# Even layer: VectorE's early operands in PSUM banks, and GLA outputs with tokens on partitions

## The reference, cut to what matters

```python
def _mix_even(h, past_k, past_v, past_ki, s0, w_in, q_norm, k_norm, rel_bias, gate_w2, gate_b2, gla_norm, w_out):
    q, k, v, qi, ki, wi, qb, kb, vb, rb, ab = _split(h @ w_in, EVEN_SIZES)
    q = _rmsnorm(q.reshape(bsz, L, A_HEADS, A_HEAD_DIM), q_norm)
    k = _rmsnorm(k.reshape(bsz, L, A_HEADS, A_HEAD_DIM), k_norm)
    ...
    o_a = _dsa_attention(...)                  # top-k selection, softmax, values
    log_alpha = jax.nn.log_sigmoid((ab @ gate_w2 + gate_b2).astype(jnp.float32)) / B_GATE_TAU
    o_b, s_new = _gla_chunked(qb * (B_KEY_DIM ** -0.5), kb, vb, log_alpha, s0, min(CHUNK, L))
    o_b = _rmsnorm(o_b.astype(h.dtype), gla_norm).reshape(bsz, L, B_VW) * jax.nn.silu(rb)
    out = jnp.concatenate([o_a.reshape(bsz, L, A_W), o_b], axis=-1) @ w_out
```

## Time and profile before

| | us |
|---|---|
| median of three runs | 1477.51 |
| lowest, highest | 1476.26, 1480.02 |
| the profiled execution | 1478.12 |
| its span in the trace | 1476.4 |
| PE busy in the span | 1423.6 (96%) |
| DVE, ACT, POOL busy | 896.6, 597.5, 370.6 |

### The profile page before, as it was taken

One profiled execution on the slowest core, in us unless ns is written; L12 is line 12 of the kernel. 1 busy time (PEld: TensorE's weight loads), 2 busy tenths in 40 slices (PEclk: granted clock), 3 DMA queues, 4 the chain that ended last, 5 costly groups with the idle time before them and its releaser, 6 DMA issues.

```text
span 1476.4 us, 25253 instructions
## 1 busy us (share of the span) xinstructions
PE 1423.6 (96%) x9708; PEld 1389.8 (94%) x9708; DVE 896.6 (61%) x1403; ACT 597.5 (40%) x975; POOL 370.6 (25%) x344
## 2 busy tenths in 40 slices
PE   7999999999779999999999999999999889999998
PEld 7999999999658999999999999989999779999998
DVE  5666655678755666655666655667565456666542
ACT  5333324446443433332433332558433544333322
POOL 4000024766415100012100003637766232000000
PEclk9999999999789999999999999989999999999999
DMA  7655951344202555864455684122222222555751
GB/s 186 179 158 146 285 146 42 116 129 139 87 3 87 143 144 157 210 178 97 123 158 145 167 228 117 58 86 87 59 85 58 90 85 82 155 157 147 185 149 44
DMA packets 324028, 188.23 MB, mean 127 GB/s; under 512 B 10954, under 2 KB 321352, under 8 KB 323964
## 3 DMA queue, kind: packets, MB, share of 16 engines
q1 hardware_dynamic: 322080, 183.22, 45.0%
q0 software_dynamic: 1216, 3.98, 0.9%
q10 hardware_dynamic: 668, 0.15, 0.1%
HBM read 183.22 MB, written 4.11 MB: 127 GB/s over the span
## 4 chain that ended last, share of the span: by engine, by line
PE 89%; DVE 6%; ACT 3%; issue 1%; DMA 1%; SPq 0%; ACTq 0%
PE PS L620 21%; PE PS L621 21%; PE PS L622 21%; PE PS L725 2%; PE PS L726 2%; PE PS L727 2%; PE PS L1193 2%; PE PS L1176 2%; PE PS L746 1%; PE PS L748 1%; PE PS L747 1%; PE PS L698 1%; PE PS L699 1%; PE PS L700 1%; DVE RA L2099 1%
## 5 line engine op out<-in xcount | busy, mean ns | idle before, releaser
L620 PE MATMUL PS<-h_hi,w_parts 128*128 128x320 f32 x1408 | 438.2, 311 | 7.1 <-DVE h_lo L1907 4.1
L621 PE MATMUL PS<-h_lo,w_parts 128*128 128x320 f32 x1408 | 436.4, 310 | 0.0
L622 PE MATMUL PS<-h_hi,w_parts 128*128 128x320 f32 x1408 | 436.3, 310 | 0.0
L620 PEld LDWEIGHTS PS<-h_hi,w_parts 128*128 128x128 f32 x1408 | 265.5, 189 | 8.8 <-issue 7.4
L621 PEld LDWEIGHTS PS<-h_lo,w_parts 128*128 128x128 f32 x1408 | 265.5, 189 | 0.3
L622 PEld LDWEIGHTS PS<-h_hi,w_parts 128*128 128x128 f32 x1408 | 265.4, 189 | 0.0
L1339 ACT ACTIVATE w_parts<-gu 128x1024 fp32r<-128x1024 f32 x176 | 176.6, 1050 | 158.4 <-PE PS L622 154.8
L620 PE MATMUL PS<-act_hi,w_parts 128*128 128x320 f32 x704 | 217.7, 309 | 0.0
L622 PE MATMUL PS<-act_hi,w_parts 128*128 128x320 f32 x704 | 217.6, 309 | 0.0
L621 PE MATMUL PS<-act_lo,w_parts 128*128 128x320 f32 x704 | 217.6, 309 | 0.0
L1895 DVE TENSOR_TENSOR w_parts<-gu,w_parts 128x1024 fp32r<-128x1024 f32 x176 | 209.1, 1229 | 3.4 <-ACT w_parts L1339 3.3
(11 more groups left out here) (386 smaller groups left out, 2380.5 us busy)
## 6 DMA issues: line engine op xcount, KB each, us to landing
gu<-in_ffn_w_gate SPq DMA_DIRECT2D x88, 512.0 KB, 4.0
gu<-in_ffn_w_up SPq DMA_DIRECT2D x88, 512.0 KB, 5.2
dn<-in_ffn_w_down SPq DMA_DIRECT2D x32, 1408.0 KB, 7.0
gu<-in_od_w_in SPq DMA_DIRECT2D x32, 512.0 KB, 5.0
gu<-in_ev_w_in SPq DMA_DIRECT2D x26, 512.0 KB, 4.8
dn<-in_ev_w_out SPq DMA_DIRECT2D x4, 1024.0 KB, 6.3
dn<-in_od_w_out SPq DMA_DIRECT2D x4, 1024.0 KB, 5.4
RB<-bias_rows POOLq DMA_DIRECT2D x2, 576.0 KB, 6.1
```

What stands on the lines that cost most here:

```text
L620: mm(out, w_hi, hi, start=first, stop=False)
L621: mm(out, w_hi, lo, start=False, stop=False)
L622: return mm(out, w_lo, hi, start=False, stop=last)
```

## The change

Two groups of edits, both in the even layer.

First, operands move from SBUF to PSUM. ScalarE's reciprocal roots stay in banks 4 to 7, where the sums were; VectorE reads them there for q and for k. VectorE's combined gate goes to banks 4 and 5, and the ten running sums read it there. Since the banks are held longer, three waits of TensorE change: `head_sums(4)` waits for the eight pieces of q, `gate()` for the four of k, `scores(0)` for `g_args`.

Second, `gla_outputs` swaps the two operands of each product, so that tokens (two heads by 64) are on partitions and the 128 features in columns. ScalarE squares each of the ten blocks from PSUM with an accumulated sum into `gcol`; the copy to `oT`, `gla_sums` and `gla_spread` are gone. VectorE scales the blocks by `gcol` (one instruction of 128x1280 into `o_rows`), TensorE turns them (ten transposes, `gla_turns`), and after `heads_out(3)` VectorE multiplies by gain and gate in four instructions (`gla_gated`). The factor 0.5 of the silu goes into the root (scale 0.25).

```diff
@@ TensorE @@
                     if l == 9:
-                        head_sums(4, s["qk_read"], 1)
+                        head_sums(4, s["q_ready"], 8)
...
             def gate():
-                pe.wait_ge(s["qk_read"], 2)
+                pe.wait_ge(s["k_ready"], 4)
...
-                        mm(PS[:, u * P:(u + 1) * P], vp[:, u, :], km_bd[:, p, c, :], start=True, stop=False)
-                        ins = mm(PS[:, u * P:(u + 1) * P], Sg(c if c < 4 else 5)[:, p, :], qe_bd[:, p, c, :],
+                        mm(PS[:, u * P:(u + 1) * P], km_bd[:, p, c, :], vp[:, u, :], start=True, stop=False)
+                        ins = mm(PS[:, u * P:(u + 1) * P], qe_bd[:, p, c, :], Sg(c if c < 4 else 5)[:, p, :],
                                  start=False, stop=True)
...
-                def gla_sums():
-                    pe.wait_ge(s["gsq"], 1)
+                def gla_turns():
+                    pe.wait_ge(s["o_rows"], 1)
                     for u in range(10):
-                        ins = mm(bank(2)[:, 256 + u:257 + u], o_squares[:, u * P:(u + 1) * P], ones[:, 0:1], start=True, stop=True)
-                    ins.then_inc(s["gsum"], 1)
-
-                def gla_spread():
-                    pe.wait_ge(s["grstd"], 1)
-                    pe.wait_ge(s["go_evac"], 2)
-                    for u in range(10):
-                        ins = mm(PS[:, u * P:(u + 1) * P], gcol[:, u:u + 1].to_broadcast([P, P]), ident[:, :],
-                                 start=True, stop=True)
-                    ins.then_inc(s["gspread"], 1)
+                        ins = tr(PS[:, u * P:(u + 1) * P], o_rows[:, u, :], ident[:, :])
+                    ins.then_inc(s["gturned"], 1)
...
-                        pe.wait_ge(s["gate_used"], 1)
+                        pe.wait_ge(s["g_args"], 1)
...
-                            pe.wait_ge(s["gnormed"], 1)
+                            pe.wait_ge(s["ob_ready"], 4)
@@ ScalarE @@
-                        rsqrt(view(rs, 0, 4, T), banks(4, 4, T), 1.0 / A_D, (s["qk_read"], 1)).then_inc(s["qk_rstd"], 1)
+                        rsqrt(banks(4, 4, T), banks(4, 4, T), 1.0 / A_D, (s["qk_read"], 1)).then_inc(s["qk_rstd"], 1)
...
-                    sc.wait_ge(s["go_evac"], 2)
-                    act_(o_squares, oT[:, 4:8, :].rearrange("p k t -> p (k t)"), ACT.Square).then_inc(s["gsq"], 1)
+                    for u in range(10):
+                        ins = act_(o_squared[:, u, :], PS[:, u * P:(u + 1) * P], ACT.Square, accum_out=gcol[:, u:u + 1])
+                    ins.then_inc(s["gsum"], 1)
...
-                    act_(gcol, gcol, ACT.Sqrt).then_inc(s["grstd"], 1)
+                    act_(gcol, gcol, ACT.Sqrt, scale=0.25).then_inc(s["grstd"], 1)
@@ VectorE @@
-                                  rs[h, p * T:(p + 1) * T].rearrange("p (c t) -> p c t", t=CH)[:, :, ::-1], ALU.mult, ALU.mult)
+                                  bank(4 + p, T)[h, :].rearrange("p (c t) -> p c t", t=CH)[:, :, ::-1], ALU.mult, ALU.mult)
...
-                    stt(pr[:, T_K + p, :], pr[:, T_K + p, :], cols[:, C_KN:C_KN + 1], k_rstd[:, p, :],
+                    stt(pr[:, T_K + p, :], pr[:, T_K + p, :], cols[:, C_KN:C_KN + 1], bank(4 + p, T),
                         ALU.mult, ALU.mult).then_inc(s["k_ready"], 1)
...
-                link(stt(gx, gx, 0.0, gx2, ALU.min, ALU.subtract))
+                link(stt(banks(4, 2, T), gx, 0.0, gx2, ALU.min, ALU.subtract))
...
-                        ins = ve.tensor_tensor_scan(gB[:, p, w], ones[:, 0:CH], gx[:, p, w], 0.0, ALU.mult, ALU.add)
+                        ins = ve.tensor_tensor_scan(gB[:, p, w], ones[:, 0:CH], bank(4 + p, T)[:, w], 0.0, ALU.mult, ALU.add)
...
-                    link(ts(gcol, bank(2)[:, 256:266], 1.0 / B_V, EPS, ALU.mult, ALU.add))
+                    link(ts(gcol, gcol, 1.0 / B_V, EPS, ALU.mult, ALU.add))
...
+                    ve.wait_ge(s["grstd"], 1)
+                    tt(o_rows, PS[:, 0:1280].rearrange("p (u e) -> p u e", e=P), gcol.unsqueeze(2).to_broadcast([P, 10, P]),
+                       ALU.mult).then_inc(s["o_rows"], 1)
+
+                def gla_gated():
+                    ve.wait_ge(s["gturned"], 1)
...
                 probs(3)
                 gla_out()
                 heads_out(3)
+                gla_gated()
```

32 lines of the change are left out of this document (13 added, 19 removed).

## The result

| | before | after |
|---|---|---|
| median of 20 runs, us | 1477.23 | 1480.08 |
| lowest, highest | 1476.26, 1480.02 | 1478.63, 1482.61 |
| profiled execution, span | 1478.12, 1476.4 | 1482.61, 1480.9 |

The ratio of the times is 1.0018, with a 95% interval of 1.0012 to 1.0025. The changed kernel is 2.85 us slower, where 2.3 us faster was forecast. The profiled execution of after is the highest of its 20, 2.5 us over its median, where that of before is 0.9 us over its own, so the two traces differ by 4.5 us and the medians by 2.85.

What follows compares the result with a forecast made beforehand. TensorE was taken as the bound, with VectorE's chain releasing its 5.30 us wait. Terms of -1.4 us up to `gla_scores` and -0.9 us in the GLA outputs gave -2.3 us: median 1475.2 us, range 1469.5 to 1483.0.

Steps and rivals of the forecast that it cites:

- part 1: q pieces: 3.85 us instead of 11.21; TensorE stalls 4.4 us, low clock costs 1.5, load 10 starts 5.9 us late.
- part 2: k pieces: they end at 358.0; TensorE waits 1.1 us at the gate; loads 12 and 13 end 7.0 us late.
- part 3: Gate: combination 0.8 us, ten sums 1.9 instead of 6.08; `g_args` at 375.6, 0.65 us earlier.
- part 4: Behind the gate to `gla_scores`: collision loss of 1.5 us offset by 1.5 elsewhere, then 1.4 us gained by the clock.
- part 5: GLA outputs: squares at 0.39 us each; third product of `scores_sample` 0.9 us earlier, range -1.8 to +1.5.
- 15.5 us saved on VectorE: VectorE's total saving up to `g_args`: 7.4 at q, 4.1 and 4.0 us after it, of which 0.65 us is left.
- early elsewhere: Behind the gate: 1.5 us that VectorE or TensorE is early, set against 1.5 us of VectorE meeting L2662.
- clock gain of 1.4 us: At `gla_scores` and the updates: full clock back after 6 us of dense scores and turns; 0 to 4 us gain, 1.4 taken.
- Rival (b): Scores and row turns behind the pause run at half rate; +4.6 us, 1482.1; chance 0.15.
- Rival (c): An operand in PSUM does not free VectorE from GpSimd; TensorE waits 11.8 us for q; +10, 1487.5; chance 0.07.
- Rival (a): q's stall is paid back in full, clock high through `gla_scores` and `gla_updates`; -6.4 us, 1471.1; chance 0.23.

Runs made afterwards that it cites:

- e2_gla: The kernel before with only the GLA outputs changed, all VectorE operands in SBUF as before; 1477.00 us, ratio 0.9995 to before.
- e1_operands: The kernel before with only the operands of q, k and gate sums in PSUM and TensorE's three waits; 1481.42 us, ratio 1.0029 to before.

## Why the prediction failed

The sum said -2.3 us. Read as distances from the start of q, the sample's logits came 4.4 us late, so 6.7 us were missed. Rounded, they are 1.4 in part 1, 1.6 in part 2, 0.1 in part 3, 1.3 in the waits of part 4, 1.7 in its clock, 0.7 in part 5.

**Part 1, q.** The pieces took 0.575 us, not 0.48, so the stall was 4.97, not 4.4, and the head sums began 5.2 us late. TensorE reaches the gate 7.3 us late, with 5.9 forecast. The low clock lasted until about 344.5 us and cost 2.0 us in this execution, where 1.5 was taken and 1.7 was the upper end; over ten traces it is 1.3 to 2.0, so 1.5 was fair. Mechanism right, stall under-sized.

**Part 2, k.** The wait was 1.18 us (1.1 forecast). No price at all was put on the clock behind it, and no reason was given; it was 1.6 us. This is the step that failed first. With part 1's error the projections end 10.3 us late and not 7.0. ScalarE's copy of load 12 ends at 370.8, and the combination starts at 373.53 where 370.4 was forecast. Taking k alone out of the changed kernel brings the combination 3.1 us forward. The prediction saw VectorE's idle time ahead of it, yet went on to count k among the "15.5 us saved on VectorE", without asking for k alone what its wait buys: 4 us less work on an engine that then idles 9.64 us.

**Part 3, gate.** Durations were right: combination 0.83, sums 1.89, and the second difference met `biased` (1.89, so 1.1 more, 1.0 taken). `g_args` came at 378.95, 3.3 us behind the forecast, about half of it from part 1 and half from part 2's clock. Nor was the gain the gate sums' own: with q alone they take 1.93 us from SBUF.

**Part 4.** The first logits wait 1.26 us for the scores where 0.5 was taken, and the small instruction waits 2.2 us for L2656, where 1.5 was taken and set off against 1.5 "early elsewhere". Nothing was early elsewhere. From `g_args` on the chain to `gla_scores` took 13.05 us against 11.8 forecast. The clock gain of 1.4 us did not come, and that is the second step that failed: the prediction took scores and turns for one dense stretch directly ahead of `gla_scores`, but `value_turns` and `key_turns` stand between, behind waits of 1.7 and 1.8 us for ScalarE. The clock fell at 389 us, in the second of these waits. L894 ran at 0.50 as before, and with L901 it took 8.0 us against 7.7.

**Part 5, GLA outputs.** Squares from PSUM at 0.25 us each, below both bounds (0.39 and 0.6). `probs(3)` starts 1.4 us earlier behind its scores, as forecast (1.3). Behind it `values(3)` took 2.62 us, since it ran at the low clock, and the wait for the gating was 1.19. Of 0.9 us forecast some 0.2 are left, in e2_gla against before as in after against e1_operands.

**The rivals.** Rival (b) came closest in time, 1482.1, and at the right clock, but at another place: not scores and row turns ran slow (3.33 and 2.78 us, full clock), but loads 10 and 12 and then `gla_scores`. Rival (c) is out: with one operand in PSUM every piece took its own length beside GpSimd's work. Rival (a) is out too. A rival with its own place at k, the wait for an operand that no one needs early, was missing.

By the Trainium skill's rule on the cost of a PSUM operand (page "VectorE: DVE Perf Modes", section on the TRN2 errata) the prediction had the sum 1.0 us worse; its own estimate for the 22 instructions was 1.4, and it doesn't say what became of the rest. For k's pieces the rows don't bear the rule out: 1.92 / 4 = 0.48 us with an operand in PSUM, 0.487 with both in SBUF. The pieces of q took 0.575; they are of 64 partitions and read both operands backwards, and no run separates the two. The rule on whole-instruction waits (page "SBUF — State Buffer", section "SBUF: two separate sides") agrees with these traces for two operands in SBUF: the second difference took 1.89 us beside L2647 and 0.82 alone. Beyond the case that the prediction took from it, VectorE's instruction of four elements a partition, with one tensor operand in SBUF and none in PSUM, took 2.40 us beside L2656, and the reduction of 128x256 just ahead of it, beside the same L2656, no more than its usual 0.42.
